# PEER decoder layer: three of four chunks of V copied, six raw slots and three row slots in the down projection

## The reference

```python
h = x @ w_in + b_in                        # x: (256, 2048) f32
A = silu(LN_c(causal_dwconv31(a_val * sigmoid(a_gate))))
S = sc_b * causal_dwconv3(sc_c * sc_h)
x1 = layer_norm(ALPHA * x + concat(A, S) @ w_out + b_out)
q = x1 @ w_q                               # 8 heads, two halves of 128
s = q . sub_keys                           # 128 keys a half
# top 16 of each half, top 16 of the 256 sums; expert = i1 * 128 + i2 (16384 experts)
act = gelu(x1 . peer_u[experts])           # 8 * 16 experts a token
f = sum(act * softmax(top_s) * peer_v[experts])
out = layer_norm(ALPHA * x1 + f)
```

## Time and profile before

| what | value |
|---|---|
| median of 3 runs | 1885.39 us (1883.87 to 1888.76) |
| the profiled execution | 1880.05 us, its span 1878.2 us |
| mean granted TensorE clock | 0.987 of full speed |
| busy, share of the span | PE 1792.3 us (95%), DVE 1366.5 (73%), ACT 852.6 (45%), POOL 416.8 (22%) |
| DMA | 568.05 MB, mean 302 GB/s |
| first and last copy issued | 33.6 us, 1191.9 us |

### The profile page before, as it was taken

The page is one execution under the profiler, slowest core; times in us unless marked ns, Lnnn a source line. Parts: engine busy times, 40 slices in busy tenths (PEclk is TensorE's granted clock), DMA queues, the critical chain, the costliest instruction groups (busy, mean ns, idle before and its releaser), DMA issues.

```text
span 1878.2 us, 31945 instructions
## 1 busy us (share of the span) xinstructions
PE 1792.3 (95%) x12082; PEld 1632.6 (87%) x12082; DVE 1366.5 (73%) x1891; ACT 852.6 (45%) x1208; POOL 416.8 (22%) x234
## 2 busy tenths in 40 slices
PE   7989899799999999999999999999999899999997
PEld 7989887599999999999999999988777687777775
DVE  7789886569974677777776444457878788878876
ACT  5434335344444444444444444444445444444443
POOL 0000004468894000000000000033444352222101
PEclk9999999999999999999999999999999999999999
DMA  8999898989989999999999999979899999999874
GB/s 274 308 299 290 270 305 260 316 266 292 288 281 303 308 297 292 308 310 299 291 295 298 314 314 311 312 227 332 337 374 357 360 362 350 337 350 348 298 228 135
DMA packets 196386, 568.05 MB, mean 302 GB/s; under 512 B 35344, under 2 KB 35472, under 8 KB 186512
## 3 DMA queue, kind: packets, MB, share of 16 engines
q1 hardware_dynamic: 167072, 494.20, 81.6%
q0 software_dynamic: 11344, 67.67, 9.3%
q10 hardware_dynamic: 17888, 5.26, 1.2%
HBM read 558.05 MB, written 142.61 MB: 373 GB/s over the span
## 4 chain that ended last, share of the span: by engine, by line
PE 40%; DMA 34%; DVE 11%; ACT 6%; issue 6%; POOL 2%; DVEq 0%; POOLq 0%; ACTq 0%; SPq 0%
DMA raw<-in_u_w_dram 16%; DMA raw<-in_v_w_dram 9%; PE psum L1425 8%; PE psum L1426 8%; PE psum L1427 8%; DVE w_lo L836 6%; DMA raw<-in_w_in_dram 6%; ACT w_hi L598 4%; PE psum L1592 3%; PE psum L1593 3%; PE psum L1594 3%; PE psum L1596 3%; PE psum L1597 3%; POOL w_lo L521 2%; DVE picked L1297 2%
## 5 line engine op out<-in xcount | busy, mean ns | idle before, releaser
L598 ACT ACTIVATE w_hi<-raw 128x1024 fp32r<-128x1024 f32 x652 | 691.3, 1061 | 937.5 <-DMA raw<-in_u_w_dram 259.0
L836 DVE TENSOR_TENSOR w_lo<-raw,w_hi 128x1024 fp32r<-128x1024 f32 x568 | 691.0, 1227 | 371.3 <-ACT w_hi L598 361.8
L1425 PE MATMUL psum<-xt_hi,w_hi 128*128 128x256 f32 x2944 | 834.3, 283 | 35.6 <-DVE w_lo L836 15.1
L1426 PE MATMUL psum<-xt_lo,w_hi 128*128 128x256 f32 x2944 | 826.9, 281 | 0.0
L1427 PE MATMUL psum<-xt_hi,w_lo 128*128 128x256 f32 x2944 | 826.3, 281 | 0.0
L1425 PEld LDWEIGHTS psum<-xt_hi,w_hi 128*128 128x128 f32 x2944 | 558.4, 190 | 42.2 <-issue 17.6
L1426 PEld LDWEIGHTS psum<-xt_lo,w_hi 128*128 128x128 f32 x2944 | 558.5, 190 | 0.0
L1427 PEld LDWEIGHTS psum<-xt_hi,w_lo 128*128 128x128 f32 x2944 | 558.2, 190 | 0.0
L552 POOL DMA_INDIRECT rows<-v_rows,sp_idx x64 | 106.8, 1668 | 922.2 <-DMA v_rows<-in_v_w_dram 615.6
L521 POOL TENSOR_TENSOR w_lo<-raw,w_hi 128x1024 fp32r<-128x1024 f32 x82 | 210.8, 2583 | 86.4 <-ACT w_hi L598 85.8
L1592 PE MATMUL psum<-w_hi,c_hi 128*128 128x512 f32 x504 | 203.5, 404 | 20.6 <-DVE w_lo L836 17.9
(11 more groups left out here) (182 smaller groups left out, 1148.6 us busy)
## 6 DMA issues: line engine op xcount, KB each, us to landing
v_rows<-in_v_w_dram SPq DMA_DIRECT2D x256, 512.0 KB, 9.4
raw<-in_u_w_dram SPq DMA_DIRECT2D x256, 512.0 KB
raw<-in_v_w_dram SPq DMA_DIRECT2D x256, 512.0 KB
raw<-in_w_in_dram SPq DMA_DIRECT2D x80, 512.0 KB
raw<-in_w_out_dram SPq DMA_DIRECT2D x32, 512.0 KB
raw<-in_w_q_dram SPq DMA_DIRECT2D x32, 512.0 KB
act_spill<-stage ACTq DMA_DIRECT2D x32, 128.0 KB, 10.1
xt_raw<-in_x_t_dram SPq DMA_DIRECT2D x4, 512.0 KB, 8.0
```

What stands on the lines that cost most here:

```text
L598: nc.scalar.activation(parts_of(slot_u)[0][:, :], raw[:, slot_u % RAW, :], ACT.Copy).then_inc(hi_done, 1)
L836: tt(lo_w[:, :], raw[:, slot_u % RAW, :], hi_w[:, :].bitcast(f32), ALU.subtract).then_inc(lo_done[slot_u % SPLIT], SPLIT)
L1425: mm(dst, hi_w[:, sl], xt_hi[:, kk, :], start=st, stop=False)
L1426: mm(dst, hi_w[:, sl], xt_lo[:, kk, :], start=False, stop=False)
```

## The change

1. `v_rows` holds the first three chunks of each expert only (1536 columns, JOINED = 3), so 192 copies are issued instead of 256, from unit 24 (instead of 12) to unit 392.
2. The fourth chunk of a picked row is gathered by a second indirect DMA, straight from peer_v's units (`v_ends`, rows of 512 columns). `selections` computes its row numbers with nine more DVE instructions.
3. `rows` has three slots instead of four. The 8 KB per partition of `rows3` become two more raw slots (`raw_late`); from the fifth down unit on (U_DEEP = 404) the loads go round six slots, and a load waits for w_lo of the unit six before it. The slots of w_hi and w_lo stay four.

```diff
--- before.py
+++ after.py
@@ -32,7 +32,7 @@
 NB = TD // BATCH
 HALVES = P // SPARSE
 PICKS = HEADS * TOPK // HALVES
-ROWS = 4
+ROWS = 3
 PICKS_IN = 16
 PART_OF_TILE = 6
 STAGE = 12
@@ -104,8 +104,34 @@
-V_UNITS = 2 * NCH * GROUPS
-COPY0, COPY1 = 12, U_DOWN - 8
+RAW_LATE = 2
+RING = RAW + RAW_LATE
+U_DEEP = U_DOWN + RAW
+
+
+def raw_slot(u):
+    return (u - U_DEEP) % RING if isinstance(u, int) and u >= U_DEEP else u % RAW
+
+
+def raw_loads(u):
+
+    before = U_DEEP // RAW if raw_slot(u) < RAW else 0
+    return before + (u - U_DEEP) // RING + 1
+
+
+def raw_before(u):
+
+    if u < U_DEEP:
+        return u - RAW
+    if u - RING >= U_DEEP:
+        return u - RING
+    return u - RAW if raw_slot(u) < RAW else None
+
+
+
+JOINED = NCH - 1
+V_UNITS = 2 * JOINED * GROUPS
+COPY0, COPY1 = 24, U_DOWN - 8
 def pick_unit(k):
@@ -174,7 +200,8 @@
         down1 = ExitStack()
         c_sets += [coefs(f"c{i}", down1) for i in (1, 2)]
-        rows_late = [sb(f"rows{i}", [P, D], f32, down1) for i in (2, 3)]
+        rows_late = [sb("rows2", [P, D], f32, down1)]
+        raw_late = sb("raw_late", [P, RAW_LATE, HALF * P], f32, down1)
         down1.close()
         xt_hi = sb("xt_hi", [P, KT, T], f32r)
         xt_lo = sb("xt_lo", [P, KT, T], f32r)
...
@@ -261,7 +292,9 @@
         picked = sb("picked", [P, D], f32)
         sp_sel = sb("sp_sel", [P, 3, PICKS], f32)
         sp_row = sb("sp_row", [P, 3, PICKS], f32)
-        sp_idx = sb("sp_idx", [P, 2, PICKS], u32)
+        sp_u = sb("sp_u", [P, 3, PICKS], u32)
+        sp_f = sb("sp_f", [P, 3, PICKS], f32)
+        sp_idx = sb("sp_idx", [P, 3, PICKS], u32)
         sp_act = sb("sp_act", [P, PICKS], f32)
         sp_coef = sb("sp_coef", [P, PICKS], f32)
         sp_tok = sb("sp_tok", [P, 2], f32)
@@ -271,8 +304,10 @@
         act_dram = nc.dram_tensor("act_spill", [N_KEYS * N_KEYS * SPARSE, 1], f32, kind="Internal").ap()
         act_tiles = act_dram.rearrange("(c p t) o -> p c (t o)", c=N_KEYS, p=P, t=SPARSE)
-        v_rows = nc.dram_tensor("v_rows", [N_KEYS * N_KEYS, D], f32, kind="Internal").ap()
+
+        v_rows = nc.dram_tensor("v_rows", [N_KEYS * N_KEYS, JOINED * DCH], f32, kind="Internal").ap()
         v_rows_of = v_rows.rearrange("(p g e) (j c) -> p g e j c", p=P, e=2, c=DCH)
+        v_ends = v_w.rearrange("u p (e c) -> (u p e) c", c=DCH)
         psum = ctx.enter_context(nc.psum_tensor("psum", [P, 8, DCH], f32))
         bank = [psum[:, i, :] for i in range(8)]
...
@@ -421,11 +456,14 @@
         @block.sync
         def _(sp):
-            def load(slot, src, u=None):
-
-                if u is not None:
-                    wait_lo(sp, u - RAW, slot)
-                sp.dma_start(raw[:, slot, :], src).then_inc(raw_in[slot], 16)
+            def load(u, src):
+                if u >= RAW:
+                    before = raw_before(u)
+                    if before is None:
+                        sp.wait_ge(used, USED0 + U_DOWN)
+                    else:
+                        wait_lo(sp, before, before)
+                sp.dma_start(raw_of(u), src).then_inc(raw_in[raw_slot(u)], 16)
             def load_x(c):
                 sp.dma_start(xt_raw[:, 4 * c:4 * c + 4, :], x_t[:, 4 * c:4 * c + 4, :]).then_inc(xt_in[c], 16)
@@ -441,8 +479,9 @@
             def copy_unit(n):
-                g, j, h = n // (2 * NCH), n // 2 % NCH, n % 2
-                sp.dma_start(v_rows_of[:, 2 * g + h, :, j, :], v_w[n].rearrange("p (e c) -> p e c", c=DCH))\
+                g, j, h = n // (2 * JOINED), n // 2 % JOINED, n % 2
+                sp.dma_start(v_rows_of[:, 2 * g + h, :, j, :],
+                             v_w[2 * NCH * g + 2 * j + h].rearrange("p (e c) -> p e c", c=DCH))\
                     .then_inc(v_copied[n % 2], 16)
             def copies_by(u):
...
@@ -550,8 +589,11 @@
                 elif k >= 2:
                     pool.wait_ge(used, USED0 + U_DOWN)
                 nc.gpsimd.indirect_dma_start(
-                    rows[k % ROWS][:, :], None, v_rows,
+                    rows[k % ROWS][:, 0:JOINED * DCH], None, v_rows,
                     bass.IndirectOffsetOnAxis(sp_idx[:, 1, k:k + 1], 0)).then_inc(rows_in[k % ROWS], 16)
+                nc.gpsimd.indirect_dma_start(
+                    rows[k % ROWS][:, JOINED * DCH:D], None, v_ends,
+                    bass.IndirectOffsetOnAxis(sp_idx[:, 2, k:k + 1], 0)).then_inc(rows_in[k % ROWS], 16)
             def gather_acts(first, end):
                 for k in range(first, end):
@@ -590,12 +632,15 @@
         def _(act):
             def hi(u, slot_u):
-                act.wait_ge(raw_in[slot_u % RAW], 16 // RAW * (u - slot_u % RAW) + 16)
+                if isinstance(u, int) and u >= U_DEEP:
+                    act.wait_ge(raw_in[raw_slot(u)], 16 * raw_loads(u))
+                else:
+                    act.wait_ge(raw_in[slot_u % RAW], 16 // RAW * (u - slot_u % RAW) + 16)
                 if isinstance(u, int) and u >= U_END - SPLIT:
                     act.wait_ge(clo_done, 2 * 26)
                 elif not isinstance(u, int) or u >= SPLIT:
                     act.wait_ge(used, USED0 + u - (SPLIT - 1))
-                nc.scalar.activation(parts_of(slot_u)[0][:, :], raw[:, slot_u % RAW, :], ACT.Copy).then_inc(hi_done, 1)
+                nc.scalar.activation(parts_of(slot_u)[0][:, :], raw_of(slot_u), ACT.Copy).then_inc(hi_done, 1)
             def x_hi(c):
                 act.wait_ge(xt_in[c], 16)
...
@@ -1267,17 +1312,32 @@
                 dve.wait_ge(sp_in, 32)
                 dve.wait_ge(tok_done, 1)
                 dve.wait_ge(fold_made, 3)
+                then(nc.vector.tensor_copy(sp_u[:, 0, :], sp_sel[:, 1, :]))
                 then(ts(sp_tok[:, 1:2], sp_tok[:, 0:1], float(SPARSE), -float(SPARSE), ALU.is_ge, ALU.mult))
                 then(stt(sp_row[:, 1, :], sp_sel[:, 0, :], float(N_KEYS), sp_sel[:, 1, :], ALU.mult, ALU.add))
                 dve.wait_ge(sp_chain, n[0])
                 then(tt(sp_tok[:, 0:1], sp_tok[:, 0:1], sp_tok[:, 1:2], ALU.add))
+                then(nc.vector.tensor_single_scalar(sp_u[:, 1, :], sp_u[:, 0, :], 1, ALU.bitwise_and))
+                then(nc.vector.tensor_single_scalar(sp_u[:, 2, :], sp_u[:, 0, :], 2, ALU.bitwise_and))
                 dve.wait_ge(sp_chain, n[0])
+                then(nc.vector.tensor_single_scalar(sp_u[:, 0, :], sp_u[:, 0, :], N_KEYS - GROUP, ALU.bitwise_and))
+                dve.wait_ge(sp_chain, n[0])
+                then(nc.vector.tensor_copy(sp_f[:, :, :], sp_u[:, :, :]))
+                dve.wait_ge(sp_chain, n[0])
+
+                then(stt(sp_row[:, 2, :], sp_f[:, 0, :], float(2 * NCH * 2 * P // GROUP), sp_f[:, 1, :],
+                         ALU.mult, ALU.add))
                 then(stt(sp_row[:, 0, :], sp_sel[:, 1, :], float(P * SPARSE), sp_tok[:, 0:1].to_broadcast([P, PICKS]),
                          ALU.mult, ALU.add))
                 dve.wait_ge(sp_chain, n[0])
+                then(stt(sp_row[:, 2, :], sp_f[:, 2, :], float(P), sp_row[:, 2, :], ALU.mult, ALU.add))
                 then(stt(sp_row[:, 0, :], sp_sel[:, 0, :], float(SPARSE), sp_row[:, 0, :], ALU.mult, ALU.add))
                 dve.wait_ge(sp_chain, n[0])
-                nc.vector.tensor_copy(sp_idx[:, :, :], sp_row[:, 0:2, :]).then_inc(idx_done, 1)
+                then(stt(sp_row[:, 2, :], sp_sel[:, 0, :], 2.0, sp_row[:, 2, :], ALU.mult, ALU.add))
+                dve.wait_ge(sp_chain, n[0])
+                then(nc.vector.tensor_scalar_add(sp_row[:, 2, :], sp_row[:, 2, :], float(2 * JOINED * 2 * P)))
+                dve.wait_ge(sp_chain, n[0])
+                nc.vector.tensor_copy(sp_idx[:, :, :], sp_row[:, 0:3, :]).then_inc(idx_done, 1)
             def pick_coefs(n):
                 sl = slice(PICKS_IN * n, PICKS_IN * (n + 1))
@@ -1289,7 +1349,7 @@
                 if k % PICKS_IN == 0:
                     pick_coefs(k // PICKS_IN)
                 dve.wait_ge(coef_done, k // PICKS_IN + 1)
-                dve.wait_ge(rows_in[k % ROWS], 16 * (k // ROWS + 1))
+                dve.wait_ge(rows_in[k % ROWS], 32 * (k // ROWS + 1))
                 if k == 0:
                     i = ts(picked[:, :], rows[0][:, :], sp_coef[:, 0:1], None, ALU.mult)
                 else:
```

More of the change, by code:

```diff
@@ L244, in build, with raw_of @@
         down2.close()
+        def raw_of(u):
+            slot = raw_slot(u)
+            return raw[:, slot, :] if slot < RAW else raw_late[:, slot - RAW, :]
         def parts_of(u):
@@ L301, in build @@
         USED0, GLU0, S0, TAPS0 = 1, 2, 2, 1
-        raw_in = [sem(f"raw_in{i}") for i in range(RAW)]
+        raw_in = [sem(f"raw_in{i}") for i in range(RING)]
         hi_done = sem("hi_done")
@@ L454, in stream @@
                     u = base + n
-                    load(n % RAW, src[n], u)
+                    load(u, src[n])
                     for m in range(copies_by(u), copies_by(u + 1)):
@@ L489, in _ @@
                         u = down_unit(g, j) + h
-                        load(u % RAW, v_w[2 * NCH * g + 2 * j + h], u)
```

(3 more changed lines are left out.)

## The result

The changed kernel takes **1803.28 us** (median of 4 runs, 1799.76 to 1805.25), the kernel before 1885.52: ratio 0.956 (95% interval 0.954 to 0.958), 82 us faster. The forecast was 1850 us with a range of 1830 to 1872: the sign was right, the forecast gain (35 us) less than half of the real one. No rival reached it either; the fastest, C, stood at 1824.

The account below looks back on a forecast made before the run. PE was taken to bound the longest stage, late loads to stall others; 10 + 1 + 2 + 4 + 17 + 1 = 35 us off 1880.05 gave 1845, or 1850 us as median of runs, range 1830 to 1872.

Parts of the forecast that it names:

- C: Whole kernel: every term at its upper end, 61 us won, 1824 us; chance 0.11.
- PE's pace as the floor: Every stage: matmul count times 0.1163 us, or 0.233 us in the down projection, is the time PE needs.
- Rival D: Down projection: gathered rows come late and picks hold up w_lo; 61 us lost, 18 won, 1928 us; chance 0.07.
- rival B: Down window: DMA keeps 351 GB/s and 499 us, 18 us won elsewhere, 1867 us; chance 0.20.
- the 358 GB/s of the Trainium skill: Down window: a rule against, memory binding at about 358 GB/s per core; 489 us, 10 us won instead of 17.
- POOL's second gathers: Down window: 62 more indirect DMAs, 104.5 us of POOL time, hidden because 200 us of idle time stay.
- the nine index steps: Stage from 581 us on: nine small DVE steps, at worst 2 us beside PE, counted as nothing.
- level: First stage, last 56 units of w_in: DMA 159 us against PE 156 us, so stalls shrink but stay; 10 us won.
- 10 + 1 + 2 + 4 = 17: Copies' gains in us by stage: 36 to 245, 245 to 458, 458 to 581 and 581 to 1196 us.
- my upper bound of 12.7: First stage, 36 to 245 us: at most 8.7 us of waits and about 4 of clock to be had.
- a pause of DVE: First stage: an unexplained DVE pause of 5.94 us, behind which PE waits 5.6 us, was assumed to stay.
- six slots: Down projection: six raw slots give a load 11.7 us instead of 7; 17 us won in the window, 1 after 1765 us.

Follow-up runs that it names:

- 130 rows: Kernel before with v_rows at 130 instead of 128 rows of 8 KB per partition, four more copies filling the new rows: 1836.09 us, ratio 0.976.
- rows by key: Kernel before with v_rows reordered as row = key * 128 + partition, without padding: 1836.24 us, ratio 0.953 on its chip.

## Why the forecast was wrong

**What held.** The two halves act in separate stages and add up within the noise. PE's pace as the floor was right to 0.2%: 0.1163 and 0.233 us a matmul are what the three windows above now take. Rival D was not seen, and rival B fell: the down window moves 367 GB/s with slices up to 393. For the 358 GB/s of the Trainium skill (page "DMA: Bandwidth & Descriptors", section "Where 436 GB/s comes from") the measurement decides against a wall in this kernel on one core. The picks' DVE, POOL's second gathers (in the window POOL idles 144 us before the first parts, where it idled 306) and the nine index steps cost nothing.

**The step that failed: the price of DMA work.** "46.7 MB, at the stage's 294 GB/s 159 us. PE needs 56 x 2.79 = 156 us. The two are level, so stalls shrink but don't all go." 294 GB/s was the rate of a stage whose DMA was saturated, at a share of 0.96, and I took it for what the DMA can do. The 3.10 us a MB was a mean that holds such stages too. Two runs show what was there in its place. With fewer copies in the old layout PE already gets 163 of its 206 missing matmuls back from 36 to 220 us, at 293 GB/s and a share of 0.91, and by unit 392 the run is 40.0 us ahead, where I had 10 + 1 + 2 + 4 = 17 and at the upper ends 32. So "level" was wrong for the copies removed alone. Without the distance of 1024 KB, with all copies, the stage moves 337 GB/s at 0.93, and PE misses none. The stage won 24.6 us against 10, and even my upper bound of 12.7 was passed.

The bound kept 5.6 us for a pause of DVE "that nothing in the trace explains". It is at the same instruction in each of these traces: 5.9 us before, 6.8 in the run with slots alone, 4.4 with 130 rows, 3.7 with rows by key, 2.9 after and 2.7 with three chunks alone. It is longest where the DMA is fullest, but does not follow the share strictly (rows by key has 0.96 in that stage), and its cause is not shown. At 4.4 us and below, PE had no wait for w_lo in that stage at all, so the pause stayed behind PE's lead: this was no fixed cost. And the clock went with the waits: 0.97 to 1.00 in that stage.

**The same in small:** from 245 to 1196 us I had 1 + 2 + 4 us, since the waits of the layer norms and of oh2g stood out. 27 us came there, 11.1 of them in the stages of w_out and w_q, whose matmuls I never counted and whose upper end I had put at 4. PE's waits by name add up to less than its missing matmuls, and I gave the difference to work that would stay. Counting matmuls had already shown 10.2 + 5.5 us missing from 458 us on; the named waits explained only a part of it, and the upper ends would have been the better choice there.

**Mis-sized only: six slots.** 17 us in the window and 1 behind it, measured 27.6 in the whole down projection, and 31.5 there in the trace of the run with the slots alone. I kept 9 us back since the DMA's 473 us stood level with PE's 473. In truth the share rose to 0.96 at 367 GB/s and PE no longer waited for w_lo. Two rates that are level on average did not stall each other with six slots in between; with four they did.

**The layout was not seen at all.** The diff shows v_rows' new width, and I priced it as bytes. That the same line moved the partitions' pieces from 1024 to 768 KB apart was no term and no rival. With all copies kept, another layout gave 48 us by itself; three chunks, which are fewer copies and another layout at once, gave 49. The trace of before could not show it by the landing of the copies, 9.4 us at a share of 0.99, since most of that was the full DMA.

## What to carry to other kernels

A transfer rate read from a saturated stage is not the DMA's capacity. Before a mean "us per MB" is used as a price, look whether the access pattern itself is cheap: here two unused rows per partition, which moved the 2 KB pieces of a copy from 1024 to 1040 KB apart, gave back 48 us of 1884. When a change moves the load and the addresses at once, a run for each is needed to tell them apart. When a diff changes a buffer's shape in HBM, work out the distance between what is written together, before and after. And where PE's missing matmuls exceed the waits that name another cause, assume that they belong to the resource at its limit.

## What was not expected of the hardware

- With the 2 KB pieces of a copy from HBM to HBM 1024 KB apart, SP's whole queue cost 3.10 us a MB, loads included, and 2.81, 2.88 and 2.85 at 1040, 8 and 768 KB. At the same rate, 280 and 282 GB/s, the share was 0.88 with 1024 KB and 0.83 with 768 KB, on two chips.
- Copies of 512 KB landed in a median of 9.4 us with 256 of them at 1024 KB, in 6.3 us up to 1145 us with 192 paced over the same units at 1024 KB, and in 5.8, 5.9 and 5.3 us at 1040, 8 and 768 KB.
- The price of the 1024 KB layout differs between chips, or between the places that the buffers get there: 1884 to 1886 us on three of them, 1929 us on one, where the changed kernel took 1801.16 us, 2 less than in the first.
- The granted clock of the whole run rose from 0.987 to 0.997 with the stalls gone.
